# All of x loaded and scaled before the adaLN sums, modulation rows and conv taps moved, narrower level products, first FFN projections by groups

## What is computed

```python
cond = silu(c)
sh1, sc1, gt1, sh2, sc2, gt2 = split(cond @ w_ada + b_ada, 6)
h = rms_norm(x, g_pre_mix) * (1 + sc1) + sh1
cv_val, cv_gate, q, f, i, og = split(h @ w_in)
out_a = silu(layer_norm(causal_depthwise_conv31(cv_val * sigmoid(cv_gate))))
out_b = rms_norm(hgrn2(silu(q), f, i)) * silu(og)        # 4 heads x 128, a gated linear recurrence
x = x + gt1 * rms_norm(concat(out_a, out_b) @ w_out, g_post_mix)
h2 = rms_norm(x, g_pre_ffn) * (1 + sc2) + sh2
gate, up = split(h2 @ w_ffn_in)                            # 2 x 2816 columns
x = x + gt2 * rms_norm((silu(gate) * up) @ w_ffn_out, g_post_ffn)
```

## Time and profile before

| | before |
|---|---|
| median of 3 runs | 1274.8 us (1274.18 to 1275.1) |
| the profiled execution's own time | 1275.91 us |
| its span | 1274.2 us |
| PE busy in the span | 1218.1 us |
| DVE busy | 594.8 us |
| POOL busy | 435.1 us |
| ACT busy | 282.4 us |
| DMA moved | 89.79 MB |
| opening (to the first piece of the periods) | 0 to 81.7 us |
| periods | 81.7 to 434.6 us |
| output projection, up to the first FFN pair's second half | 434.6 to 551.7 us |
| rest of the first pair, and the FFN | 551.7 to 1274.2 us |

### The profile page before, as it was taken

How to read it: one execution, slowest core, us unless ns; L and a number is a source line. 1 busy time by engine, 2 the same in 40 slices (tenths; PEclk the granted TensorE clock), 3 DMA queues, 4 the chain that set the end, 5 groups by cost and what they waited for, 6 DMA issues and landing times.

```text
span 1274.2 us, 14573 instructions
## 1 busy us (share of the span) xinstructions
PE 1218.1 (96%) x5820; PEld 1020.9 (80%) x5820; DVE 594.8 (47%) x725; ACT 282.4 (22%) x417; POOL 435.1 (34%) x236
## 2 busy tenths in 40 slices
PE   3699999999989999989999999999999999999997
PEld 3678888888878878868888888888888888888875
DVE  4665969979697664631414141313131222222227
ACT  5345144261432624320000000000000000000003
POOL 3115326153243540323332424141424242424235
PEclk9899999999989999989999999999999999999999
DMA  9524224142230150111110212121212121111103
GB/s 332 150 66 132 84 67 132 34 120 79 67 99 17 51 198 1 50 33 50 32 57 28 65 33 66 33 66 33 66 33 66 33 66 33 55 44 49 49 17 132
DMA packets 91833, 89.79 MB, mean 70 GB/s; under 512 B 2733, under 2 KB 80786, under 8 KB 91794
## 3 DMA queue, kind: packets, MB, share of 16 engines
q1 hardware_dynamic: 91488, 89.14, 22.5%
q10 hardware_dynamic: 306, 0.12, 0.0%
HBM read 85.05 MB, written 4.19 MB: 70 GB/s over the span
## 4 chain that ended last, share of the span: by engine, by line
PE 89%; DVE 5%; ACT 2%; issue 2%; POOL 2%; DMA 1%; SPq 0%; DVEq 0%; POOLq 0%; ACTq 0%
PE pair L1312 53%; PE pair L1419 24%; PE pair L1347 3%; PE pair L1274 1%; PE pair L1477 1%; DVE pair L953 1%; PE pair L1259 1%; POOL wo_lo L457 1%; DVE acc L832 1%; ACT w_hi L543 1%; DMA x<-in_x 1%; POOL wo_hi L455 1%; PE pair L1361 1%; PE pair L1223 1%; PE pair L1363 0%
## 5 line engine op out<-in xcount | busy, mean ns | idle before, releaser
L506 POOL CAST w_hi<-raw 128x1024 fp32r<-128x1024 f32 x60 | 65.3, 1089 | 438.3 <-PE pair L1312 253.9
L1157 DVE TENSOR_TENSOR ufull<-gate,pair 128x1024 f32<-128x1024 f32 x22 | 26.9, 1221 | 387.9 <-PE pair L1312 374.4
L1312 PE MATMUL pair<-ha_hi,w_hi 128*128 128x512 f32 x512 | 164.2, 402 | 1.9 <-ACT sg L616 1.9
L953 DVE SCALAR_TENSOR_TENSOR pair<-u,conv_w_col,pair 128x512 f32<-128x512 f32 x240 | 162.4, 750 | 1.3 <-DVE state L1036 0.2
L1312 PE MATMUL pair<-hb_hi,w_hi 128*128 128x512 f32 x512 | 161.8, 397 | 0.0
L1312 PE MATMUL pair<-ha_lo,w_hi 128*128 128x512 f32 x512 | 159.8, 394 | 0.0
L1312 PE MATMUL pair<-ha_hi,w_lo 128*128 128x512 f32 x512 | 159.1, 392 | 0.0
L1312 PE MATMUL pair<-hb_lo,w_hi 128*128 128x512 f32 x512 | 158.2, 390 | 0.0
L1312 PE MATMUL pair<-hb_hi,w_lo 128*128 128x512 f32 x512 | 157.9, 390 | 0.0
L508 POOL TENSOR_TENSOR w_lo<-raw,w_hi 128x1024 fp32r<-128x1024 f32 x60 | 151.4, 2523 | 4.8
L1171 DVE TENSOR_TENSOR yt<-yt,pair 128x1024 f32<-128x1024 f32 x80 | 97.7, 1221 | 112.5 <-PE pair L1419 112.0
(11 more groups left out here) (213 smaller groups left out, 1588.1 us busy)
## 6 DMA issues: line engine op xcount, KB each, us to landing
ada<-in_w_ada SPq DMA_DIRECT2D x48, 512.0 KB, 4.1
raw<-in_w_ffn_in SPq DMA_DIRECT2D x44, 512.0 KB, 3.9
raw<-in_w_in SPq DMA_DIRECT2D x24, 512.0 KB, 3.8
raw<-in_w_ffn_out SPq DMA_DIRECT2D x22, 512.0 KB, 3.3
x<-in_x SPq DMA_DIRECT2D x8, 512.0 KB, 8.3
raw<-in_w_out SPq DMA_DIRECT2D x8, 512.0 KB, 3.2
x<-in_x SPq DMA_DIRECT2D x4, 1024.0 KB, 8.1
out<-x SPq DMA_DIRECT2D x8, 512.0 KB, 2.6
```

Source lines behind the costliest of these rows:

```text
L506: pool.tensor_copy(w_hi[:, j % WS, :], raw[:, j % RAW, :]).then_inc(loop_hi, 1)
L953: i_ = dve.scalar_tensor_tensor(out=dst, in0=src, scalar=w, in1=dst, op0=ALU.mult, op1=ALU.add)
L1157: dve.tensor_tensor(ufull[:, :], gate[:, :], pair[1][:, :], ALU.mult).then_inc(ufull_ready, 1)
L1312: i_ = pe.matmul(dst[:, cols], w, x[:, cols], start=first and s_ == 0, stop=last and s_ == 2)
```

## The change

1. x is loaded first, all eight tiles, then ada block 0, then the first two weight chunks. All eight tiles are squared and scaled in place (`normalise_x`) ahead of ada block 0's sums. `turn_x` turns the scaled tiles with PE transposes by the identity, not with products by diagonals. The DVE and PE orders after it are rewritten by hand, and POOL splits weight chunk 2 after the last ada block's sums and not after the squares.
2. `SLOTS` and both `PLACES` put M behind the first S; `ada_rows` names earlier chunks (one earlier for the first modulation, two for the others); the last period has none.
3. Of the taps, 44 and not 37 of the last channel tile come before its period ends, 26 up to piece 32.
4. In the S slots only the keys that a level reads are loaded as weights: 128 less the level's length. `place` copies as many partitions.
5. The second token half of the first FFN pair goes by rows kt: each row's six matmuls (gate and up) wait for that row only, and the transposes of later rows stand between them.

```diff
-SLOTS = ["VT", "VT", "DIAG", "DIAG"] + ["S"] * 7 + ["M", "KDT", "KDT", "C", "C", "O", "O", "OT", "OT"]
+SLOTS = ["VT", "VT", "DIAG", "DIAG", "S", "M"] + ["S"] * 6 + ["KDT", "KDT", "C", "C", "O", "O", "OT", "OT"]
-PLACES_LAST = [0, 0, 3, 4, 6, 8, 9, 11, 13, 14, 16, 17, 18, 19, 20, 21, 24, 25, 30, 31]
+PLACES_LAST = [0, 0, 3, 4, 6, 7, 8, 9, 11, 13, 14, 16, 18, 19, 20, 21, 24, 25, 30, 31]
-TAPS_FIRST = 37
+TAPS_FIRST = [37, 37, 37, 44]
+TAPS_EARLY = 26
 def ada_rows(g):
-    t, c = divmod(g - 3, 5)
-    return [KT * t + 2 * c, KT * t + 2 * c + 1] if 0 <= t < 4 and c < 4 else []
+    t, c = divmod(g - 1, 5) if g > 5 else (0, g - 2)
+    return [KT * t + 2 * c, KT * t + 2 * c + 1] if t < 4 and 0 <= c < 4 else []
...
+            for i in range(TT):
+                sp.dma_start(x0[:, i, :], x_d[:, i, :]).then_inc(x_loaded[i], 16)
             load_block(0)
-            for i in range(TT):
-                if i == 4:
-                    for g in range(RAW):
-                        load_chunk(g)
-                sp.dma_start(x0[:, i, :], x_d[:, i, :]).then_inc(x_loaded[i], 16)
+            for g in range(RAW):
+                load_chunk(g)
...
             for g in range(2):
                 split_at(g)
-            pool.wait_ge(ss_ready, TT)
+            pool.wait_ge(acc_ready, KT // 2)
             split_at(2)
...
-            def norm_diagonal(i):
+            def normalise_x(i):
                 dve.wait_ge(ss_ready, i + 1)
-                me.done(dve.reciprocal(rs[:, 0, i:i + 1], rs[:, 0, i:i + 1]))
-                me.wait()
-                dve.tensor_scalar(diag[:, i, :], ident[:, :], rs[:, 0, i:i + 1], None, ALU.mult).then_inc(xs_ready, 1)
+                normalise(x0[:, i, :], x0[:, i, :], i, 0).then_inc(xs_ready, 1)
+            for i in range(TT):
+                normalise_x(i)
+            other_vectors()
             sum_rows(0, range(KT))
-            for i in range(4):
-                norm_diagonal(i)
             scale_shift(0)
             scale_shift(1)
-            other_vectors()
             low_half(0)
             low_half(1)
-            for i in range(4, TT):
-                norm_diagonal(i)
-            sum_rows(1, range(4))
+            sum_rows(1, range(2))
             low_half(2)
-            sum_rows(1, range(4, 6))
+            sum_rows(1, range(2, 4))
             low_half(3)
-            sum_rows(1, range(6, KT))
+            sum_rows(1, range(4, KT))
...
-                    i_ = pe.matmul(group_bank(g)[:, i * P:(i + 1) * P], x0[:, 4 * half + i, kt * P:(kt + 1) * P],
-                                   diag[:, 4 * half + i, :], start=True, stop=True)
+                    i_ = pe.transpose(group_bank(g)[:, i * P:(i + 1) * P], x0[:, 4 * half + i, kt * P:(kt + 1) * P],
+                                      ident[:, :])
...
                 elif kind == "S":
                     pe.wait_ge(level, 8 * t + half + 1)
+                    rows = P - (1 << half)
                     for i in range(TT):
-                        i_ = pe.matmul(dst[:, i * 64:(i + 1) * 64], qk[:, 1, cols(i)],
+                        i_ = pe.matmul(dst[0:rows, i * 64:(i + 1) * 64], qk[:, 1, i * P:i * P + rows],
                                        right(qk[:, 0, cols(i)], 1 << half), start=True, stop=True)
...
+            for kt in range(KT):
+                pe.wait_ge(h_ready, 16 + 8 + kt + 1)
                 for n in range(2):
-                    if half == 0:
-                        pe.wait_ge(w_split, F0 + n + 1)
-                        pe.wait_ge(tail_read, TT - 1 + n)
-                    elif n == 0:
-                        pe.wait_ge(h_ready, 32)
-                    i_ = project_half(pair[n], (F0 + n) % WS, half)
+                    i_ = project_part(pair[n], (F0 + n) % WS, kt, 1)
...
+                if 13 + kt < 16:
+                    turn_tiles(1, xs, [13 + kt])
```

More of the change, by code:

```diff
@@ L588, in full_and_high @@
                 act.activation(dst, full0[:, g % 2, :], ACT.Copy).then_inc(hi_ready, 1)
-            squares(range(4))
-            for g in range(2):
-                full_and_high(g)
-            squares(range(4, TT))
-            for g in range(2, 16):
+            squares(range(TT))
+            for g in range(16):
                 full_and_high(g)
@@ L958, in taps @@
                 if period < 4 and piece > U_AT:
-                    per = TAPS_FIRST
-                    a, b = ((piece - U_AT - 1 + x) * per // (39 - U_AT) for x in (0, 1))
+                    early, per = TAPS_EARLY, TAPS_FIRST[period]
+                    a, b = (min(x, 16) * early // 16 + max(x - 16, 0) * (per - early) // 7
+                            for x in (piece - U_AT - 1, piece - U_AT))
                     base = 2 * TAPS * period
@@ L965, in taps @@
                         return
-                    per = 2 * TAPS - TAPS_FIRST
-                    a, b = ((piece + x) * per // length for x in (0, 1))
-                    base = 2 * TAPS * (period - 1) + TAPS_FIRST
+                    done = TAPS_FIRST[period - 1]
+                    a, b = ((piece + x) * (2 * TAPS - done) // length for x in (0, 1))
+                    base = 2 * TAPS * (period - 1) + done
                 for n in range(base + a, base + b):
@@ L1277, in project_group @@
                         i_.then_inc(w_used, 1)
+            pe.wait_ge(vec_loaded, 16 * VEC_LOADS)
+            pe.wait_ge(vec_ready, 1)
+            pe.transpose(bank(7)[:, 0:ROWS], rows_a[:, :], ident[0:ROWS, 0:ROWS])
+            pe.transpose(bank(7)[:, P:P + TAPS * CT], rows_b[:, :], ident[0:TAPS * CT, 0:TAPS * CT]).then_inc(vec_turned, 1)
             mod_sums(0)
@@ L1290, in _ @@
             turn_x(3)
-            project_group(2)
+            for g in range(3):
+                project_group(g)
             mod_sums(2)
+            mod_sums(3)
             project_group(3)
             turn_x(4)
-            mod_sums(3)
             turn_x(5)
@@ L1467, in _, with project_part @@
             F0 = N_IN + N_OUT
-            def project_half(dst, slot, half):
+            def project_part(dst, slot, kt, half):
                 cols = slice(half * HALF, (half + 1) * HALF)
-                for kt in range(KT):
-                    hi, lo = (ha_hi, ha_lo) if kt < 4 else (hb_hi, hb_lo)
-                    w = slice(kt * P, (kt + 1) * P)
-                    wh, wl = w_hi[:, slot, w], w_lo[:, slot, w]
-                    for s_, (a, x) in enumerate([(wh, hi), (wh, lo), (wl, hi)]):
-                        i_ = pe.matmul(dst[:, cols], a, x[:, kt % 4, cols], start=kt == 0 and s_ == 0,
-                                       stop=kt == KT - 1 and s_ == 2)
+                hi, lo = (ha_hi, ha_lo) if kt < 4 else (hb_hi, hb_lo)
+                w = slice(kt * P, (kt + 1) * P)
+                wh, wl = w_hi[:, slot, w], w_lo[:, slot, w]
+                for s_, (a, x) in enumerate([(wh, hi), (wh, lo), (wl, hi)]):
+                    i_ = pe.matmul(dst[:, cols], a, x[:, kt % 4, cols], start=kt == 0 and s_ == 0,
+                                   stop=kt == KT - 1 and s_ == 2)
                 return i_
@@ L1502, in down @@
                         i_.then_inc(w_used, 2)
-            for half in range(2):
-                for n in range(2):
-                    if half == 0:
-                        pe.wait_ge(w_split, F0 + n + 1)
-                        pe.wait_ge(tail_read, TT - 1 + n)
-                    elif n == 0:
-                        pe.wait_ge(h_ready, 32)
-                    i_ = project_half(pair[n], (F0 + n) % WS, half)
-                    if half:
+            pe.wait_ge(w_split, F0 + 1)
+            pe.wait_ge(tail_read, TT - 1)
+            for kt in range(KT):
+                project_part(pair[0], F0 % WS, kt, 0)
+            turn_tiles(1, xs, range(8, 11))
+            pe.wait_ge(w_split, F0 + 2)
+            pe.wait_ge(tail_read, TT)
+            for kt in range(KT):
+                project_part(pair[1], (F0 + 1) % WS, kt, 0)
+                if kt % 4 == 3:
+                    turn_tiles(1, xs, [11 + kt // 4])
+            for kt in range(KT):
+                pe.wait_ge(h_ready, 16 + 8 + kt + 1)
+                for n in range(2):
+                    i_ = project_part(pair[n], (F0 + n) % WS, kt, 1)
+                    if kt == KT - 1:
                         i_.then_inc(w_used, 1)
-                    else:
-                        turn_tiles(1, xs, range(8 + 4 * n, 12 + 4 * n))
+                if 13 + kt < 16:
+                    turn_tiles(1, xs, [13 + kt])
             with pe.Fori(0, FB - 1) as bk:
```

35 lines of the change are left out of this document (16 added, 19 removed).

## The result

| | before | after | after, measured again |
|---|---|---|---|
| median | 1274.95 us of 4 runs | 1257.41 us of 4 (1255.55 to 1258.15) | 1255.66 us of 5 (1251.82 to 1258.74) |
| ratio to before, 95% interval | | 0.9861 [0.9844, 0.9878] | 0.9845 [0.9824, 0.9866] |
| profiled execution: span | 1274.2 us | 1255.6 us | 1252.7 us |
| first piece of the periods | 81.70 | 81.20 | 79.28 |
| first level of the last head | 364.86 | 359.93 | 356.41 |

The change saves 17.5 us where 15.3 were forecast (1274.8 to 1259.5), and the time lies inside the range. Set against before's marks, the first profiled execution was 0.5 us ahead at the first piece, 4.9 at the last head, 13.7 at the output projection and 18.9 at the FFN loop.

What follows compares the result with a forecast made beforehand. PE, busy 96% of the span, was taken as the bound. Terms 0.9 + 5.2 + 5.8 + 3.8 = 15.7 us from 1275.9 gave 1260.2, about 1259.1 as median; forecast 1259.5, range 1252 to 1267.

Steps and rivals of the forecast that it cites:

- Opening: 0.9 forecast: Before the first piece: block 0's sums end at 30, the opening at 78.9 against 79.8, so 0.9 us less.
- 13.1 us to block 1's: Opening: interval from the end of block 0's sums to the end of block 1's, forecast at 13.1 us.
- 10.9 and 10.4 forecast: Opening: intervals to the ends of block 2's and block 3's sums, 14.8 and 13.0 us before.
- PE's last one: Opening after block 3's sums: PE is the bound, 14.5 us forecast against 15.3 before.
- the bound for 25.7: Opening: if no POOL instruction stands between block 0's sums, they end at 25.7, giving 4 us less.
- Periods: 5.2 forecast: Periods 1 to 3: time goes with loaded columns, 1.7 us saved a head, 5.2 in three; bounds 0 and 5.2.
- Last period: 5.8 forecast: Last period: 5.8 us less with M, which is done inside a remaining 3 us wait before S2; bounds 3 and 10.
- then the gated head and the weight split of POOL still stand in its way: Last period: after `extend` at 368.1, POOL still delays DVE; scores are placed at 373.0 and S2 starts at 373.1.
- The bound of 10: Last period: up to 10 us saved if PE stays at the upper clock; the lower one costs some 4.4 there.
- FFN pair: 3.8 forecast: First FFN pair: 5.5 us less by rows, minus 1.7 for a clock fall: 3.8 less; bounds 2.5 and 5.5.
- the 5.5 without the clock: First FFN pair: 565.0 before less 559.5 after, 5.5 us saved before the clock fall's 1.7 is taken off.
- at 7 to 8 us less than 559.66 beyond the shift: First FFN pair, a sign of the prediction: the silu table load begins that much earlier, followed by a stand of 1.8.

## Why the prediction was right, step by step

The time is right by 2.1 us (3.8 by the second median); of the mechanism, one step failed and others erred both ways, so part of that closeness is luck.

**Opening: 0.9 forecast, 0.5 in the profiled execution.** The first half of its steps held: the chunk's landing, POOL between the sums, their end at 29.64 and 13.1 us to block 1's. The next were too short (10.9 and 10.4 forecast, 11.7 and 11.8 measured) and PE's last one too long (14.5, measured 13.0, at the upper clock from 66 us on); that they cancel is luck. And 30 was one outcome. In seven profiled executions with this order the sums ended at 26.41, 28.35, 28.37, 28.46, 28.46, 28.81 and 29.64, by when each of DVE and POOL came (the sums start between 19.66 and 20.47) and which got in first. With POOL kept away they end at 25.63 and the first piece stands at 77.20, 4.5 us ahead of before's 81.70; the bound for 25.7 was 4. The rule of the Trainium skill (SBUF — State Buffer, "Who interferes with whom"), that the one that starts first keeps the other out for its whole instruction, agrees with the rows above, in both directions; the cast that waited 1.27 us was kept out for longer than one multiply-add (4.06 / 6 = 0.68).

The sums do not decide the opening alone. The kernel with other level sizes and the one with POOL's additions back have the same code up to there. They ended the sums at 28.37 and 28.46, and had their first pieces at 78.18 and 80.02. They were still together at block 1's end (41.47 and 41.57) and 1.8 apart at block 3's (63.31 and 65.15), and the granted clock from 54 to 66 us was 1.00 in the one and 0.87 in the other. Before's opening varies as much: its first piece stood at 80.23 to 83.13 in four executions, 81.7 on average. The changed opening's stood at 78.18 to 81.20 in the six that kept the stand of 1.89 us, 79.4 on average: 2.3 us ahead, more than the 0.5 of the pair that the forecast is set against.

**Periods: 5.2 forecast, 3.8 measured.** That loaded columns and not moving ones set the time was right down to 96 columns. The term's size was wrong at 64: such an instruction takes 66 to 67 ns and not 54, whether 64 or 32 columns move, which is 0.2 us a head. The levels of 96 and 112 saved a little less than their share. The seven levels together take 10.67 us for 12.11, 1.44 less, and the period is shorter by 1.3; the last 0.15 a head is not accounted for. The Trainium skill (TensorE: Matmul & The Clock Gate, "LDWEIGHTS (loading the stationary operand)") has columns over 1.2 in ns: 107 for 128 and 80 for 96, the runs 108 for 128 and 83 for 96. For 64 it has 53, and the runs show 66 to 67; for 32 it has 27, and the runs show 65 with 64 moving columns and 37 with 32.

**Last period: 5.8 forecast, 9.4 measured** (13.7 less 4.9, and the 0.6 by which the last head's first level came sooner than the periods' gain), the term that was wrong. The failing step is "then the gated head and the weight split of POOL still stand in its way", by which "the scores are placed at 373.0". The forecast itself had DVE's product at 368.1 and read the gated head at 369.48 on before's clock, so by its own times DVE came first. DVE first is what the trace shows, 0.9 us apart, and then DVE's two products go through. No wait of 3 us follows and PE runs on. The bound of 10 was reached in five later executions, in which the clock stayed up behind the 1.11 us wait as well: 85.9 to 86.3 us against 95.95. The two experiments on this part meet from both sides: moving M and the rows alone gives 8.2, and putting four additions back takes 6.6 in this stretch (93.75 for 87.16), or 7.5 to 7.8 against those five. Executions of one code differ by some 1.1 us here (95.95 and 97.10 with before's), so the last microsecond of each is not to be read. How much of it is M's own 1.7 was not tried apart: with M late and the rows early, the next modulation's first row would have to wait for it.

**FFN pair: 3.8 forecast, 5.1 measured.** The stand (1.8, measured 1.77) and the 5.5 without the clock were right within 0.4. What failed is taking from the stand at the periods' start, behind which "it ran at 0.53 for 3.4 us", that the clock would fall here too: it was read from one execution as if it always did. Behind the stand of 1.77 the clock fell in one of eight profiled executions. The sign that the silu table load begins "at 7 to 8 us less than 559.66 beyond the shift" contradicts the prediction's own 557.1, 2.6 less; on before's clock it began at 557.5.

The errors have both signs: opening -0.4, periods -1.4, last period +3.6, FFN +1.3. They make 3.1 us more than forecast; at the loop's start the lead is 18.9 for 15.7, and the span shows 18.6.

## What to carry to other kernels

Where DVE and POOL both work from SBUF, write down which of them starts first at each crossing and by how much: 0.9 us decided over a wait of 3.4, and an instruction of POOL's that is off the path (a row added early or late) can put DVE on the wrong side. Cost a clock fall behind a stand of 1.8 us as a chance and not as a sum, and shorten the stand: what filled most of it here was a table load of 1.28 us that idle time could hold. And compare two variants of a few us by the stage that the edit touches, since here one program's own medians lay 1.8 us apart and its openings 2. Read a stage of the kernel before from several executions too: its opening alone ended anywhere in 2.9 us.

## What the runs showed of the chip that was not expected

Behind PE's stand of 1.89 us at the first piece, the granted clock fell to the lower level in 5 of 12 profiled executions and stayed at the upper in 7. Where it fell, that cost 1.6 us (48.0 to 48.1 us from the first piece to head 0's first level, against 46.4). In four of the five it came late, in the third row behind the restart and not in the first. Behind the 1.1 us of the last period it fell in 1 of 8, behind 1.77 us in 1 of 8, behind the 2.35 to 2.8 us at the output projection's restart in 11 of 14, and behind the stands of 3.4 to 5.1 us in the last period and the FFN pair in all nine. The changed kernel itself went both ways: its two profiled executions differ at the first piece and again behind the 1.77 us.

A DVE instruction with one tensor operand in SBUF and a value for each partition was also kept out by POOL: 2.41 and 2.65 us for a scaling of 0.75. The Trainium skill (SBUF — State Buffer, "Who interferes with whom") has this for DVE's two-port modes; the trace does not show the mode.
